# Start addresses of the activation region at a multiple of 256 bytes

## Time and profile before

| | us |
|---|---|
| median of three executions | 711.84 |
| lowest and highest | 711.78, 713.47 |
| the profiled execution | 712.9 |
| its span, first to last instruction | 711.1 |
| mean granted TensorE clock | 0.894 of full speed |
| TensorE matmul busy | 587.2 (83%) |
| VectorE busy | 302.8 (43%) |
| ScalarE busy | 189.7 (27%) |
| moved by DMA | 247.73 MB, mean 348 GB/s |

### The profile page before, as it was taken

How to read it: one execution, slowest core, us unless ns; L and a number is a source line. 1 busy time by engine, 2 the same in 40 slices (tenths; PEclk the granted TensorE clock), 3 DMA queues, 4 the chain that set the end, 5 groups by cost and what they waited for, 6 DMA issues and landing times.

```text
span 711.1 us, 15452 instructions
## 1 busy us (share of the span) xinstructions
PE 587.2 (83%) x6636; PEld 410.9 (58%) x6636; DVE 302.8 (43%) x626; ACT 189.7 (27%) x332; POOL 29.6 (4%) x56
## 2 busy tenths in 40 slices
PE   8999999999999999996875767776678656887584
PEld 5787899999999885553432333333334333443342
DVE  6475976985474945442222222122312222111412
ACT  4493355473535434110111001010011100110111
POOL 8003000000000020000000000000000000000000
PEclk9999999999999999998798788797877988687969
DMA  8995546536579699999999999999999999999993
GB/s 253 349 328 187 163 137 203 175 121 213 175 274 420 234 395 369 427 425 428 425 427 425 426 429 427 426 427 427 425 425 428 427 427 427 424 426 427 423 417 146
DMA packets 39619, 247.73 MB, mean 348 GB/s; under 512 B 4360, under 2 KB 6496, under 8 KB 25472
## 3 DMA queue, kind: packets, MB, share of 16 engines
q1 hardware_dynamic: 38096, 245.44, 85.6%
q0 software_dynamic: 912, 1.25, 1.0%
q10 hardware_dynamic: 544, 0.06, 0.1%
HBM read 245.67 MB, written 1.06 MB: 347 GB/s over the span
## 4 chain that ended last, share of the span: by engine, by line
PE 50%; DMA 44%; SPq 1%; another core or an unknown queue 1%; DVE 1%; issue 1%; ACT 0%; ACTq 0%; DVEq 0%
DMA wide<-in_w_expert_up 38%; PE ps L1366 8%; PE ps L1029 6%; PE ps L1030 6%; PE ps L1031 6%; DMA wide<-in_w_expert_down 3%; PE ps L1401 3%; PE ps L1002 3%; PE ps L1004 3%; PE ps L1003 3%; PE ps L1325 2%; DMA ring<-in_w_in 2%; PE ps L1413 1%; PE ps L1381 1%; SPq L526 1%
## 5 line engine op out<-in xcount | busy, mean ns | idle before, releaser
L1366 PE MATMUL ps<-wide,xe 128*32 128x256 f32 x2048 | 162.1, 470 | 109.3 <-DMA wide<-in_w_expert_up 109.3
L1366 PEld LDWEIGHTS ps<-wide,xe 128*32 128x32 f32 x2048 | 75.9, 131 | 176.9 <-issue 132.1
L1882 DVE TENSOR_TENSOR xe<-ps,g_ffn 128x256 f32<-128x256 f32 x32 | 13.6, 425 | 258.4 <-PE ps L1334 258.4
L1486 DVE TENSOR_TENSOR ring_lo<-ring,w_hi 128x1024 fp32r<-128x1024 f32 x76 | 92.0, 1228 | 46.2 <-ACT w_hi L721 45.7
L721 ACT ACTIVATE w_hi<-ring 128x1024 fp32r<-128x1024 f32 x76 | 79.0, 1058 | 58.8 <-PE ps L1031 35.3
L1029 PE MATMUL ps<-hT_hi,w_hi 128*128 128x256 f32 x320 | 89.4, 279 | 0.2 <-DVE hT_lo L1498 0.2
L1030 PE MATMUL ps<-hT_lo,w_hi 128*128 128x256 f32 x320 | 88.4, 276 | 0.0
L1031 PE MATMUL ps<-hT_hi,ring_lo 128*128 128x256 f32 x320 | 88.4, 276 | 0.0
L925 ACT ACTIVATE he<-ps 128x128 f32<-128x128 f32 x32 | 8.9, 278 | 207.7 <-PE ps L1381 204.7
L1401 PE MATMUL ps<-wide,he 128*32 128x256 f32 x1024 | 62.5, 382 | 1.9 <-DMA wide<-in_w_expert_down 1.8
L1029 PEld LDWEIGHTS ps<-hT_hi,w_hi 128*128 128x128 f32 x320 | 60.1, 188 | 0.7 <-issue 0.7
(11 more groups left out here) (276 smaller groups left out, 785.9 us busy)
## 6 DMA issues: line engine op xcount, KB each, us to landing
wide<-in_w_expert_gate SPq DMA_DIRECT2D x27, 2048.0 KB, 45.6
wide<-in_w_expert_up SPq DMA_DIRECT2D x27, 2048.0 KB, 48.2
wide<-in_w_expert_down SPq DMA_DIRECT2D x27, 2048.0 KB, 41.1
ring<-in_w_in SPq DMA_DIRECT2D x8, 2048.0 KB, 16.1
ring<-in_w_merge_gate SPq DMA_DIRECT2D x6, 2048.0 KB, 9.6
wide<-in_w_expert_gate SPq DMA_DIRECT2D x10, 1024.0 KB, 13.2
wide<-in_w_expert_up SPq DMA_DIRECT2D x10, 1024.0 KB, 10.6
wide<-in_w_expert_down SPq DMA_DIRECT2D x9, 1024.0 KB, 11.8
```

The source lines that it names most:

```text
L1366: ins = t_.matmul(ps[q * WIN:(q + 1) * WIN, b, 0:QW], xe[b][:, k % 2, k // 2, :], w, start=(k == 0), stop=(k == KD - 1))
L1486: v.tensor_tensor(piece(ring_lo, g, c), piece(ring, g, c), by_row(out_hi[g == 19][c]).bitcast(F32), ALU.subtract).then_inc(wpre_lo, 1)
```

## The change

The activation region starts at the next multiple of 256 bytes above the small tensors. In the region, the helper `here` rounds the size of each tensor of at least 1024 bytes up to a multiple of 256, and of smaller ones to 32 as before. Only conv_u has such a size that this matters: 4128 bytes become 4352. Everything before the region keeps its address.

```diff
-        region = top[0]
+        region = (top[0] + 255) // 256 * 256 + 0
 
         def here(name, shape, dt):
-            nonlocal_at = here_at[0]
-            here_at[0] += (int(np.prod(shape[1:])) * mybir.dt.size(dt) + 31) // 32 * 32
-            return place(name, shape, dt, at=nonlocal_at)
+            at = here_at[0]
+            size = int(np.prod(shape[1:])) * mybir.dt.size(dt)
+            step = 256 if size >= 1024 else 32
+            here_at[0] += (size + step - 1) // step * step
+            return place(name, shape, dt, at=at)
```

## The result

The changed kernel takes 716.43 us (median of six, 715.4 to 717.61) against 711.9 for the kernel before (711.57 to 714.17): a ratio of 1.006, interval 1.0047 to 1.0073. It is slower, by some 4.5 us. The forecast had said no change that can be measured; the time lies just inside the range, near the price that the slower rival had.

A forecast was written before the change was run, and what follows sets the result against it. The prediction took TensorE, then the expert-weight stream, to bound the kernel in series. Only the convolution branch counted: -0.42 us on the profiled 712.9 gave 712.5, or 711.4 on the median, with a range of 707.5 to 716.5 us.

The forecast's parts named there:

- the slower rival: Dense matmul triples slow down from the new weights-to-activations distance, up to 4.8 us, 716.2 in all; chance 0.18.
- What bounds the kernel: TensorE paces the first part, the expert-weight stream the second; a microsecond saved before 250 us ends the run that much sooner.
- The convolution branch, -0.4: Its 32 triples lose 13 ns each once yc_lo leaves its offset of 32: 0.42 us less.
- offset of 32: Start of yc_lo, 32 bytes above a multiple of 256; claimed to cost 13 ns a triple in the convolution branch.
- The other 384 triples, 0: 320 hT, 32 ya and 32 yg triples going from 64 to 0: no change, between -7.7 and +4.8 us.
- The bound from above: 368 triples taking the slow pace of 106 to 111 us, 13 ns more each: +4.8 us.
- The rival with the new distance: Same as the slower rival: triples at lines 1029 to 1031 slow down, up to 4.8 us, 716.2; chance 0.18.
- Tokens on the output rows, 0: 96 triples with hT stationary and weights moving, output projection included: no change, bounds -1 to +2.5 us.
- VectorE and ScalarE, 0: Splits and rounding copies: address makes at most 1%, hidden behind the matmuls, so no change.
- The transfers, 0: Expert weights into the four slot pairs in the region: no change, bounds -1.5 to +1.5 us.
- The estimate from the rule: If the 256-byte rule for reads held for writes into expert slots: 0.6 us less.
- The sum: All terms together: -0.42 us on the profiled 712.9, 711.4 on the median.

The follow-up runs named there:

- e1: Changed kernel with the activation region 64 bytes above a multiple of 256, weights at 128: 711.31 us, ratio 0.9983 to the kernel before.
- e3: Changed kernel with the activation region 128 bytes above a multiple of 256, weights also at 128 (distance 0): 718.71 us, ratio 1.008.
- e6: Changed kernel with sizes still rounded up to 256 but the region at its old start, large activations at 32: 716.85 us, ratio 1.0063.
- e5: Changed kernel with everything ahead of the region moved up 128 bytes, so weights, ring, activations and all slots start at multiples of 256: 715.64 us.
- (0,64): Activations 0 and weights 64 bytes above a multiple of 256, the layout of e2: 710.33 us.
- (64,128): Activations 64 and weights 128 bytes above a multiple of 256, the layout of e1: 711.31 us.
- (0,0): Activations and weights both at a multiple of 256, the layout of e5: 715.64 us.
- (128,128): Activations and weights both 128 bytes above a multiple of 256, the layout of e3: 718.71 us.
- e4: Changed kernel with the activation region 192 bytes above a multiple of 256, weights at 128 (distance +64): 717.54 us, ratio 1.0073.
- e10: Changed kernel with the activation region 96 bytes above a multiple of 256, weights at 128 (distance -32): 717.69 us, ratio 1.0071.
- e9: Changed kernel with only hT put back 64 bytes above a multiple of 256, weights at 128: 713.28 us, ratio 1.0012.
- e7: e1 with the four pairs of expert slots in the region moved up to multiples of 256: 710.42 us, ratio 0.9977.
- e8: Changed kernel with weights, ring, x_tok and all eleven slot pairs at multiples of 256, activations at 192 (distance -64): 708.18 us, ratio 0.9943.
- e2: Changed kernel with everything ahead of the region moved up 192 bytes, weights at 64, region at 0 (distance -64): 710.33 us, ratio 0.998.
- e11: Changed kernel with weights, ring and x_tok at a multiple of 256, region at 192, slots not moved, seven pairs at 0: 708.86 us.

## Why the prediction was wrong

**What bounds the kernel: right.** Two parts in series, coupled one to one. The cleanest pair is e1 and e3, whose slots are all off a multiple of 256: the first expert matmul starts at 270.7 and 277.7 us, the spans are 709.0 and 716.0, 7.0 us both times. One reading was off: the 38% of the earlier trace rows are not the wait for one expert's up weights but the up-weight transfers of six experts along the chain.

**The convolution branch, -0.4: an address was the cause, but not the offset of 32 by itself.** yc at 64 instead of 32 gives 276 ns (e1) and 0.34 a triple, worth the 0.4 us. But the change moved yc to distance 128, where it has 281, and the branch became 0.1 us longer (32 x 2.4 ns). The prediction's "offset of 32" was the activation's address taken alone; with the weights at 128 it is a distance of -96, and e6 has 0.352 there for ya and yg. The branch's 0.353 is also the second pace of hT; whether yc_lo brought the branch into it was not tried. The Trainium skill's lines of 16 bytes (Advanced Engine Details and Errata, SBUF Cachelines) do not account for the pace: every start tried is a multiple of 16, and the triple ranges from 0.340 to 0.360. By that rule nothing would have changed; the measurement decides.

**The other 384 triples, 0: this step failed.** I took 0 because ya and yg, "separately placed tensors", had exactly hT's 276 ns. They stood at the same offset as hT, 64, with the weights at the same 128, so they were three readings of one case and no evidence for another. The bound from above, "if the new distance between the weights' and the activations' addresses put all of the others into it, 368 x 13 ns = +4.8 us", was the right mechanism; the price was 15 to 16 ns and not 13, since distance 128 has a pace of its own (0.356) and not hT's second pace of 0.353. Against the 0 of the forecast the runs showed 320 x 15.0 ns for hT and 32 x 16.1 and 32 x 15.9 ns for ya and yg, +5.8 us in all, set by the distance from the weights (e1 to e5). The rival with the new distance, with a chance of 0.18, is what happened, and its sign was the one named: it said 282 ns for hT, and hT has 281. Its total of 716.2 is near the measured 716.43 by luck: it held 4.8 us for these triples and nothing for the tokens and the stream.

**Tokens on the output rows, 0.** Between the bounds given (-1 to +2.5): +1.0 us. "The moving side, which is most of what is read, stays where it is, so I take 0" was the same mistake, an address taken alone where the distance counts.

**VectorE and ScalarE, 0: right,** 303.1 and 189.7 us busy against 302.8 and 189.7.

**The transfers, 0: the bound too narrow.** I allowed 1.5 us either way and the part after the dense one became 2.6 shorter, 2.0 of it by the rate. I had looked for a pattern in stretches of 5 us between slots at 128, 64 and 32, where none was, and none of them was at a multiple of 256. I also let only the four pairs that move gain; the packets show that others gained too. The Trainium skill's rule (DMA: Bandwidth & Descriptors, How a descriptor splits into AXI transactions), stated for reads, names the right boundary: 256 bytes was the one that counted here, for writes into the slots. No run shows that this is how the gain comes about. The estimate from the rule was 0.6 us less; measured by the rate it was 2.0, some three times that.

**The sum.** -0.4 forecast, +6.7 - 2.6 = +4.1 found. Two errors of opposite signs stood behind a total that moved by only 0.6%. That the time lies inside the range is luck: without the stream's gain, which the forecast did not have, it would be at some 718.4 us, 2 above the range.

## What to carry to other kernels

Where an fp32r matmul with 128 x 128 stationary bounds a stage, the start of the moving tensor relative to the stationary one, modulo 256, can be a tuning parameter: here it was worth up to 6% (0.340 to 0.360 us). Try the four multiples of 64 and look at the gap between starts in the timeline; which one is best differs between the two forms here. Where the stream of large loads bounds a stage, try their destinations at multiples of 256 bytes, independently of that (0.7% of the rate here): tensors that share memory with a load's slot needn't share its start. And when a trace is to tell what an address does, count how many different addresses its rows really have.

## What the runs showed of the hardware that I had not expected

- The pace of the matmul triples depends on the distance of the two operands, with a sign: -64 is fast with the activations moving (0.340 against 0.353 at +64), while with the weights moving distance 0 is the fastest (0.680 against 0.687 and more). The reason was not tried; only the dependence is shown. That it repeats after 256 bytes is borne out by (0,64) beside (64,128), and by (0,0) beside (128,128): in each pair of kernels hT stands 256 bytes further from, or nearer to, w_hi, and the pace is the same.
- With 16 columns stationary instead of 128 (the w_z matmuls, whose weights stand 64 above those of the ring) the medians stay at 276 or 277 ns at all four distances: 128 in the kernel before, +64 in the changed one, -64 in e3, 0 in e4. In all four most triples take 0.340. So the penalty of the 128-column tile does not show in these 8 triples. With the activations at 32 (e6) and 96 (e10) their medians too rise, to 278 to 280.
- At the good distance there is a second pace, 0.353, that was entered at a restart or after a slow branch and kept until the next interruption: 126 gaps in e9, 44 in e7 and e8, 14 in the kernel before (the 16 triples of the earlier trace rows), e2 and e11, none in e1. What picks it was not settled.
- With all expert slots at a multiple of 256 bytes, 98% of the writes of 16 KB into a partition last 611 ns; with none there only 27 to 32% last so short, and nearly all others 612 to 624 ns. The stream gains 0.7%, 426 to 429 GB/s. With four of the eleven pairs there it already has 428, and more packets are short than go into these four.
